# A two-layer transformer kernel on one core: three gate units of the first projection computed by token rows, with 512 columns to a matmul

## The reference, cut to what matters

```
h = rms_norm(x, norm_mix)                       # 256 x 1024
proj = h @ w_in                                 # 1024 x 4352
q_a, k_a, v_a, q_b, k_b, v_b, g_a, g_b = split(proj)      # g_a, g_b: 1024 columns each
o_a = neighbourhood_attention(...)              # 8 heads of 64
o_b = sliding_window_attention(...)             # 8 heads of 64, with a sink
y = sigmoid(g_a) * (o_a @ w_branch_a) + sigmoid(g_b) * (o_b @ w_branch_b)
x = x + y @ w_out
```

## Time and profile before

| | before |
|---|---|
| median of three runs | 1027.01 us (1026.66 to 1027.70) |
| the profiled execution | 1026.77 us |
| its span, first to last instruction | 1024.9 us |
| around the span | 1.87 us |
| granted TensorE clock, mean | 0.965 |
| instructions | 16692 |
| TensorE matmul, VectorE, ScalarE busy | 88%, 44%, 32% of the span |

### The profile page before, as it was taken

How to read it: one execution, slowest core, us unless ns; L and a number is a source line. 1 busy time by engine, 2 the same in 40 slices (tenths; PEclk the granted TensorE clock), 3 DMA queues, 4 the chain that set the end, 5 groups by cost and what they waited for, 6 DMA issues and landing times.

```text
span 1024.9 us, 16692 instructions
## 1 busy us (share of the span) xinstructions
PE 900.8 (88%) x7172; PEld 614.7 (60%) x7172; DVE 451.7 (44%) x579; ACT 329.4 (32%) x427; POOL 17.5 (2%) x34
## 2 busy tenths in 40 slices
PE   9999999999999999999999996777768686777876
PEld 8889988888888889979989632221313121131311
DVE  6587778688767348995776310000001000010101
ACT  5456664565455328544433400000000000000002
POOL 1400000000000000000000000000000000000000
PEclk9999999999999999999999999888999889898989
DMA  9884424576645454442358999999999999999994
GB/s 331 231 304 156 166 84 164 164 243 209 201 165 200 169 195 175 165 167 81 111 184 332 387 418 421 421 421 421 421 421 422 422 422 422 422 421 421 420 420 190
DMA packets 87735, 294.97 MB, mean 288 GB/s; under 512 B 6383, under 2 KB 33791, under 8 KB 64624
## 3 DMA queue, kind: packets, MB, share of 16 engines
q1 hardware_dynamic: 82288, 284.18, 71.9%
q10 hardware_dynamic: 3840, 6.08, 1.7%
q0 software_dynamic: 1536, 3.68, 1.3%
HBM read 290.77 MB, written 4.10 MB: 288 GB/s over the span
## 4 chain that ended last, share of the span: by engine, by line
PE 54%; DMA 34%; DVE 9%; SPq 2%; issue 1%; ACT 0%; ACTq 0%; DVEq 0%
DMA arena<-in_w_down 15%; DMA arena<-in_w_up 13%; PE psum L1213 8%; PE psum L1099 6%; PE psum L1101 6%; PE psum L1100 6%; DMA arena<-in_w_gate 5%; PE psum L1215 4%; PE psum L1834 4%; PE psum L1240 3%; PE psum L1854 3%; DVE ring_rounded L2378 3%; PE psum L1576 3%; PE psum L1060 2%; PE psum L1066 1%; PE psum L1052 1%
## 5 line engine op out<-in xcount | busy, mean ns | idle before, releaser
L1834 PE MATMUL psum<-arena,featL 128*32 128x512 f32 x1008 | 166.8, 651 | 60.6 <-DMA arena<-in_w_up 47.0
L2378 DVE TENSOR_TENSOR ring_rounded<-arena,hi_rounded 128x2048 fp32r<-128x2048 f32 x77 | 175.9, 2289 | 67.4 <-ACT hi_rounded L1968 66.4
L1968 ACT ACTIVATE hi_rounded<-arena 128x2048 fp32r<-128x2048 f32 x77 | 146.8, 1912 | 100.1 <-DMA arena<-in_w_in 23.6
L1834 PEld LDWEIGHTS psum<-arena,featL 128*32 128x32 f32 x1008 | 38.5, 117 | 176.4 <-DMA arena<-in_w_up 86.2
L1854 PE MATMUL psum<-arena,featT 128*32 128x512 f32 x488 | 100.6, 701 | 38.7 <-DMA arena<-in_w_down 33.9
L1213 PE MATMUL psum<-ffn_in_rounded,hi_rounded 128*128 128x512 f32 x352 | 122.5, 393 | 0.7 <-DVE ffn_in_rounded L2370 0.7
L1099 PE MATMUL psum<-hi_rounded,featT_rounded 128*128 128x256 f32 (+1 forms) x368 | 113.5, 308 | 3.9 <-DVE ring_rounded L2378 3.4
L1101 PE MATMUL psum<-hi_rounded,featL_rounded 128*128 128x256 f32 (+1 forms) x368 | 111.1, 302 | 0.0
L1100 PE MATMUL psum<-ring_rounded,featT_rounded 128*128 128x256 f32 (+1 forms) x368 | 111.1, 302 | 0.0
L1215 PE MATMUL psum<-ffn_in_rounded,ring_rounded 128*128 128x256 f32 x352 | 98.8, 281 | 0.0
L2899 DVE TENSOR_TENSOR featT<-featT,psum 128x512 f32<-128x512 f32 x8 | 8.2, 1028 | 192.3 <-PE psum L1834 192.3
(11 more groups left out here) (332 smaller groups left out, 1266.9 us busy)
## 6 DMA issues: line engine op xcount, KB each, us to landing
arena<-in_w_up SPq DMA_DIRECT2D x73, 1024.0 KB, 26.3
arena<-in_w_gate SPq DMA_DIRECT2D x70, 1024.0 KB, 26.5
arena<-in_w_down SPq DMA_DIRECT2D x58, 1024.0 KB, 26.9
arena<-in_w_in SPq DMA_DIRECT2D x14, 2048.0 KB, 8.1
arena<-in_w_down SPq DMA_DIRECT2D x5, 2048.0 KB, 7.8
arena<-in_w_out SPq DMA_DIRECT2D x3, 2048.0 KB, 9.0
arena<-in_w_in SPq DMA_DIRECT2D x4, 1024.0 KB, 9.2
arena<-in_w_down SPq DMA_DIRECT2D x8, 512.0 KB, 22.0
```

What stands on the lines that cost most here:

```text
L1834: ins = mm(psum[32 * j:32 * j + 32, MB[4 + m], :], xg[:, 4 * half + k, 32 * j:32 * j + 32], held(place(q, j), j, 512 * k), start=half == 0 ...
L1968: fn(high, view, ACT.Copy).then_inc(hi_ready, 1)
L2378: tt(low, view, high.bitcast(F32), ALU.subtract).then_inc(lo_ready, 1)
```

## The change

Units 6, 7 and 8 are halved by rows of the contraction like units 0 to 3; unit 5 stays divided by columns. In the attention steps 2 to 7 TensorE calls a new function, `project_rows`: step i computes row tile t = i mod 2 of unit 5 + i // 2 with all 512 columns, in 24 matmuls: the high weights of both chunks first (16 matmuls), then the low weights of chunk 0 and of chunk 1 (4 each). At t = 0 it waits for the high part and for the low part of each chunk. Since a unit's two chunks are now both read in both of its steps, high parts live longer, and there is a third place for them, W_CST: 2048 columns in the buffer of constants (the decay table and the first of the two LoRA matrices), which are loaded later, in the feed-forward stage. The order of places in the units after it is turned accordingly. ScalarE's copy out of the bank goes to one row tile with 512 columns instead of two with 256. Neither VectorE's nor ScalarE's order is changed, nor is SyncE's.

```diff
--- before.py
+++ after.py
@@ -98,6 +98,7 @@
 W_QK = place(L1["qaT"][0])
 W_NAT = (L1["nat"][0], L1["nat"][0] + NQKV)
 W_PROB, W_PROBT, W_SPARE = (place(L1[n][0]) for n in ("prob", "probT", "spare"))
+W_CST = place(-CHUNK)
 
 W_RING = (place(SLOT), place(SLOT + CHUNK), place(LM["M"][0] + CHUNK))
 W_FFN = place(LF["end"])
@@ -368,7 +369,10 @@
         xn = sb("xn", [P, NT, D])
         featT, featR = sb_rounded("featT", [P, DK, T])
         featL, featLR = sb_rounded("featL", [P, DK, T])
-        cst = sb("cst", [P, HELD["end"]])
+        cst, cst_r = sb_rounded("cst", [P, HELD["end"]])
+        dec_lo = CST["dec"][0]
+        hi_r[W_CST] = cst_r[:, dec_lo:dec_lo + CHUNK]
+        assert dec_lo + CHUNK <= HELD["lora"][1]
         lora, gup, sig_g = (cst[:, slice(*HELD[n])] for n in ("lora", "gup", "gate"))
         tanh_w = cst[0:64, slice(*HELD["tanh"])]
         cols = sb("cols", [P, COLS["end"]])
@@ -690,15 +694,17 @@
         for u in range(4):
             halves(("p1", u), (ring[2 * u % 4], ring[2 * u % 4 + 1]))
         chunk(("p1", 4), 0, cols256(("p1", 4), 0), ring[0], ("p1", 4, 0))
-        for n in range(8):
-            u, c = 5 + n // 2, n % 2
-            chunk(("p1", u), c, cols256(("p1", u), c), (W_SPARE, W_NAT)[n % 2], ("p1", u, c))
-        ring = (W_SPARE, W_NAT, W_QK, W_PROB)
+        ring = (W_SPARE, W_NAT, W_CST)
+        for c in range(2):
+            chunk(("p1", 5), c, cols256(("p1", 5), c), ring[c], ("p1", 5, c))
+        for u in range(6, 9):
+            halves(("p1", u), [ring[(2 * (u - 5) + c) % 3] for c in range(2)])
+        ring = (W_CST, W_SPARE, W_QK, W_PROB)
         for br in range(2):
             for c in range(2):
                 chunk(("br", br), c, lambda of, br=br, c=c: wview(("br", br), 0, of)[:, :, 512 * c:512 * c + 512], ring[2 * br + c],
                       ("br", br, c, 1))
-        ring = (W_SPARE, W_NAT, W_FFN, W_PROB)
+        ring = (W_NAT, W_SPARE, W_FFN, W_PROB)
         for n in range(4):
             chunk(("wo", n // 2), n % 2, cols256(("wo", n // 2), n % 2), ring[n], ("wo", n // 2, n % 2))
         ring = (W_FFN, W_PROBT, W_PROB, W_SPARE)
@@ -1151,6 +1157,29 @@
                     if c == 0:
                         ins.then_inc(half_read, 1)
 
+            def project_rows(name, t):
+
+                b = begin(*name, t)
+                for low in range(2):
+                    for c in range(2):
+                        if t == 0:
+                            if low:
+                                wait_split(pe, chunk_of[name, c])
+                            else:
+                                pe.wait_ge(hi_ready, chunk_of[name, c] + 1)
+                        for k in range(4):
+                            tile = lambda f: f[:, 4 * c + k, t * P:(t + 1) * P]
+                            if low:
+                                ins = mm(b, tile(featR), lo_cols(chunk_of[name, c], k, 0, 512), start=False,
+                                         stop=(c, k) == (1, 3), skip_group_check=True)
+                                if (t, c, k) == (1, 0, 3):
+                                    ins.then_inc(half_read, 1)
+                            else:
+                                for f in (featR, featLR):
+                                    mm(b, tile(f), hi_cols(chunk_of[name, c], k, 0, 512), start=c + k == 0 and f is featR,
+                                       stop=False, skip_group_check=True)
+                end(ins)
+
             def first_unit(name):
 
                 banks = [begin(*name, t) for t in range(NT)]
@@ -1350,7 +1379,10 @@
                     turned(i - 1)
                 if i < 8:
                     u, c = 5 + i // 2, i % 2
-                    project(("p1", u, c), ("p1", u), c)
+                    if u == 5:
+                        project(("p1", u, c), ("p1", u), c)
+                    else:
+                        project_rows(("p1", u), c)
                 if i == 0:
                     turn_qk("qb", "kb")
                 if i == 8:
@@ -2085,7 +2117,10 @@
                         ins.then_inc(exp_ready, 1)
                     u, c = 5 + i // 2, i % 2
                     wait_filled(act, "p1", u, c)
-                    ins = fn(sig[:, :, 256 * i:256 * i + 256], bank("p1", u, c).rearrange("p (t n) -> p t n", t=NT), ACT.Copy)
+                    if u == 5:
+                        ins = fn(sig[:, :, 256 * i:256 * i + 256], bank("p1", u, c).rearrange("p (t n) -> p t n", t=NT), ACT.Copy)
+                    else:
+                        ins = fn(sig[:, c, 512 * (u - 5):512 * (u - 4)], bank("p1", u, c), ACT.Copy)
                     empty(ins, "p1", u, c)
                     if i == 0:
                         qk_moved("qb", "kb")
```

## The result

The kernel with the change takes **1030.21 us** (median of 8 runs, 1029.22 to 1031.57), the kernel before beside it 1027.09 us (8 runs, 1026.25 to 1028.14). The ratio is 1.0027, 95% interval 1.0018 to 1.0036: slower by 2.8 us (the two medians lie 3.1 apart), where I had forecast 0.7 us and no change that can be told. It lies above my range.

The account below looks back on a forecast made before the run. TensorE was taken to bound steps 2 and 3, VectorE steps 4 to 7. The terms -0.02 - 0.29 + 0.50 + 0.50 = +0.7 us on 1027.01 gave 1027.7 us, range 1025.9 to 1029.0.

Parts of the forecast that it names:

- The price of a column: Gate chunks in steps 2 to 7: 24 matmuls of 512 columns save 0.29 us of TensorE per step.
- The wait in the even steps: Steps 2, 4 and 6: TensorE waits for VectorE's second low part; -0.02, +0.50 and +0.50 us.
- Steps 5 and 7: Attention steps where VectorE's chain stays as long and TensorE gets 0.3 us more slack; change 0.
- Rival 2: Steps 4 and 6: TensorE's clock falls in the new gaps; 1032 us for one, 1037 for two; one in twenty-five.
- Costed at nothing: Low parts, copies, high parts and loads around the steps add nothing; the 0.7 us goes through to the end.

Follow-up runs that it names:

- rows_nowait: The changed kernel reading the first chunk's low part again in the even steps, so without the wait for the second; 1028.51 us, ratio 1.0012.
- cols_copyfirst: The kernel before with VectorE's copy of the transposes put ahead of the low part; 1026.79 us, ratio 0.9990.
- rows_plus32: The changed kernel with 32 semaphore increments on TensorE's queue in the existing 2.7 us wait; 1028.86 us, ratio 1.0009.
- cols_minus35: The kernel before with 221 semaphore increments, two ahead of each matmul of two first-projection units, 29 in the 2.7 us wait; ratio 1.0059.
- cols_warm: The kernel before with ten extra TensorE matmuls in the 2.7 us wait; 1028.25 us, ratio 1.0005.
- cols_plus40: The kernel before with 40 semaphore increments on TensorE's queue in the 2.7 us wait; 1028.79 us, ratio 1.0012.
- rows_again: The changed kernel, unchanged, profiled and timed once more; 1031.98 us.

## Why the prediction was wrong

- **The price of a column**: right. Step 3 gained 0.23 us where I said 0.29; the rule of the Trainium skill ("TensorE: Matmul & The Clock Gate", section "Back-to-back issue gap") would have given 0.06, so the trace does not bear it out here. I had left out its condition: in that section the Trainium skill gives that rule for a matmul in isolation, and for a stream of pairs of weight load and matmul about 131 ns at 512 columns. The 227 ns here do not bear that out either.
- **The wait in the even steps**: right in place and size. -0.09, +0.43 and +0.45 us where I said -0.02, +0.50 and +0.50; TensorE stood 0.70 us in step 4 where I had 0.75. In step 2 my own numbers made no wait (the low part at 91.94, TensorE there at 92.2), and I charged one all the same; the trace shows no idle time over 0.15 us there, and rows_nowait puts its cost at 0.13. The sum was 0.55 for a forecast of 0.7, and rows_nowait took it back.
- **Steps 5 and 7**: right, 9.17 as before; and cols_copyfirst shows that VectorE's order bounded them.
- **Rival 2**, a fall of the clock in the new gaps: wrong place. The new gaps of 0.7 us did not bring it, the old one of 2.7 us did, at its old length, and at 1.5 us, not 5.
- **The step that failed** is the last sentence of "Costed at nothing": "What follows the steps depends on TensorE down to the experts' stream of weights, so that the 0.7 us goes through to the end." I had looked at what the change moves in data and time, and not at what it moves in the program. The 0.55 us did go through (at 455 us the kernel after was 0.51 behind, though it had entered step 2 0.2 ahead), and 291 instructions fewer cost 1.8 us on top (rows_plus32 gives them back; cols_minus35 makes the stretch of after in the kernel before). The clock's 1.5 us are in the two profiles in full; between the kernels they are worth less, since the kernel before has them in part of its executions. How much less stays open: two thirds of 1.5, 1.0 us, if it falls in one of three executions before and in all after (an estimate from five profiles), 0.7 by cols_warm against cols_plus40. 0.55 + 1.8 + 0.7 to 1.0 is 3.1 to 3.4 us, measured 2.8 by the ratio and 3.1 by the medians.

I also held a range of 3 us for a sum whose stretch of 400 us behind the change I had put at zero spread. The earlier trace rows had no row of the dense stretch; a look at its "issue" rows would have shown a cost that the change could move.

## What to carry to other kernels

A change that takes instructions away moves every later instruction against the 256-instruction blocks in which the program is fetched; where an engine runs through small instructions without a pause, look for "issue" idle times, count them modulo 256, and try a few dozen increments in an existing wait before judging the change. A wait of 2.7 us on TensorE can cost the clock behind it (1.5 us here); filled with cheap matmuls it did not in six of six profiles, but count the instructions that they add. Where two engines are within a few per cent of each other in a loop, first put the slower one's order right (VectorE's copy ahead of its low part, 0.9 us), for a saving on the other gives nothing where the slower one bounds the step.

## What the runs showed of the hardware that I had not expected

- At a rate of 256 instructions in 3.6 to 4 us TensorE stalls at some of the borders: 0.16 to 1.44 us, 52 of 52 at a block's border, at the same instructions each time the same kernel was profiled (rows_again had one more than after). Which borders they are goes with the position in the main, not by it alone.
- The same 2.7 us wait, at the same length, lets the granted clock fall in some executions and not in others of the same kernel (1.00, 0.83, 1.00 in three profiles of before).
- Two semaphore increments beside each matmul of 512 columns cost nothing that can be told in one function (0.231 us from matmul to matmul with and without them) and 70 ns in another (0.30 against 0.227 us); not explained.
